# GpSimd writes a weight panel's high part with a copy in place of a product with ones, its loops written out

## What is computed

```python
def reference(x, ...):
    x = first_block(x, ...)    # stick-breaking attention, SwiGLU, gated side input
    x = second_block(x, ...)   # convolution of 31 taps and retention, in parallel
    return third_block(x, ...) # S5 and SSD state-space branches, gated side input

def swiglu(x, w_in, w_out):
    a, b = jnp.split(x @ w_in, 2, axis=-1)
    return (jax.nn.silu(a) * b) @ w_out
```

## Time and profile before

| | us |
|---|---|
| median of 3 runs (4802.05 to 4804.78) | 4803.22 |
| profiled execution, its own time | 4795.22 |
| its span, from the first to the last instruction | 4793.4 |
| TensorE busy (matmuls) | 4037.3 (84%) |
| VectorE busy | 2435.2 (51%) |
| GpSimd busy | 1553.4 (32%) |
| ScalarE busy | 881.2 (18%) |

### The profile page before, as it was taken

The page is one execution under the profiler, slowest core; times in us unless marked ns, Lnnn a source line. Parts: engine busy times, 40 slices in busy tenths (PEclk is TensorE's granted clock), DMA queues, the critical chain, the costliest instruction groups (busy, mean ns, idle before and its releaser), DMA issues.

```text
span 4793.4 us, 49704 instructions
## 1 busy us (share of the span) xinstructions
PE 4037.3 (84%) x19722; PEld 3259.1 (68%) x19722; DVE 2435.2 (51%) x2518; ACT 881.2 (18%) x1502; POOL 1553.4 (32%) x581
## 2 busy tenths in 40 slices
PE   7899998999999997777888895899896875559898
PEld 6677766877877875666665574678785764447677
DVE  3555556333333549877343324545249955543555
ACT  2433434100000221110001101112110111212021
POOL 1222222655556325555422130232223420004332
PEclk9999999999999988888999996988998976669899
DMA  1000000211111101111211111111831241112111
GB/s 68 27 27 23 23 27 31 66 58 65 53 60 63 36 27 52 58 61 57 70 44 49 48 44 44 48 53 62 143 78 55 90 135 27 26 26 83 66 40 57
DMA packets 139172, 260.00 MB, mean 54 GB/s; under 512 B 45584, under 2 KB 87568, under 8 KB 135952
## 3 DMA queue, kind: packets, MB, share of 16 engines
q1 hardware_dynamic: 47376, 143.67, 10.3%
q10 hardware_dynamic: 91648, 114.21, 7.3%
HBM read 209.35 MB, written 46.14 MB: 53 GB/s over the span
## 4 chain that ended last, share of the span: by engine, by line
PE 58%; DVE 16%; issue 15%; POOL 6%; ACT 3%; DMA 2%; ACTq 0%; SPq 0%; DVEq 0%; POOLq 0%
PE bank L514 15%; PE bank L515 14%; PE bank L516 14%; POOL wh L471 4%; PE bank L622 4%; POOL wl L473 2%; PE bank L751 1%; PE bank L714 1%; DVE xl L1610 1%; DVE spill L2098 1%; DVE hn L1599 1%; DVE fb L1737 1%; PE bank L984 1%; PE bank L734 1%; DVE gl L1774 1%
## 5 line engine op out<-in xcount | busy, mean ns | idle before, releaser
L471 POOL TENSOR_TENSOR wh<-raw,mats 128x1024 fp32r<-128x1024 f32 x264 | 739.5, 2801 | 3136.3 <-PE bank L516 3085.8
L514 PE MATMUL bank<-xh,wh 128*128 128x512 f32 x3008 | 1212.0, 403 | 279.6 <-DVE apad L1847 65.1
L515 PE MATMUL bank<-xl,wh 128*128 128x512 f32 x3008 | 1192.8, 397 | 0.0
L516 PE MATMUL bank<-xh,wl 128*128 128x512 f32 x3008 | 1190.6, 396 | 0.0
L514 PEld LDWEIGHTS bank<-xh,wh 128*128 128x128 f32 x3008 | 579.0, 192 | 445.3 <-issue 175.1
L473 POOL TENSOR_TENSOR wl<-raw,wh 128x1024 fp32r<-128x1024 f32 x264 | 697.4, 2642 | 20.7
L516 PEld LDWEIGHTS bank<-xh,wl 128*128 128x128 f32 x3008 | 577.8, 192 | 124.3
L515 PEld LDWEIGHTS bank<-xl,wh 128*128 128x128 f32 x3008 | 579.2, 193 | 115.6
L1867 DVE SCALAR_TENSOR_TENSOR cacc<-apad,cols,cacc 128x1024 f32<-128x1024 f32 x232 | 346.4, 1570 | 0.0
L1737 DVE TENSOR_TENSOR_SCAN fb<-fb 128x256 f32<-128x256 f32 (+7 forms) x128 | 209.5, 1677 | 102.8 <-ACT ab L1136 102.8
L1646 DVE TENSOR_TENSOR h<-bank,h 128x512 f32<-128x512 f32 x240 | 164.8, 691 | 188.9 <-PE bank L516 188.9
(11 more groups left out here) (324 smaller groups left out, 5691.1 us busy)
## 6 DMA issues: line engine op xcount, KB each, us to landing
raw<-in_wstream SPq DMA_DIRECT2D x264, 512.0 KB, 3.5
spills<-spill ACTq DMA_DIRECT2D x40, 512.0 KB, 2.7
rawm<-in_mod_w ACTq DMA_DIRECT2D x12, 1024.0 KB, 4.8
gate_spill<-gates ACTq DMA_DIRECT2D x16, 512.0 KB, 2.6
tabs<-in_rope ACTq DMA_DIRECT2D x4, 2048.0 KB, 7.6
f<-spills ACTq DMA_DIRECT2D x8, 1024.0 KB, 8.3
h<-in_x ACTq DMA_DIRECT2D x4, 1024.0 KB, 11.1
conv_spill<-cout ACTq DMA_DIRECT2D x8, 512.0 KB, 2.7
```

What stands on the lines that cost most here:

```text
L471: nc.gpsimd.tensor_tensor(wh[:, slot], raw[:, slot], ones, ALU.mult).then_inc(S("panel_high"), 1)
L514: nc.tensor.matmul(o, lh, rh, start=start, stop=False)
L515: nc.tensor.matmul(o, lh, rl, start=False, stop=False)
L516: return nc.tensor.matmul(o, ll, rh, start=False, stop=stop)
```

## The change

The high part of a panel, and of a modulation batch, is written by a copy from float32 to F32R; the constant ones and the wait for them at GpSimd's start go. GpSimd's hardware loop over the turns of a phase becomes a Python loop, so that all its splits stand in the program as plain instructions with constant waits. What waits for what is unchanged.

```diff
             nc.gpsimd.memset(eps[:, :], EPS).then_inc(S("eps"), 1)
-            ones = M["ones"].unsqueeze(1).broadcast_to([P, KT, P])
-            pool.wait_ge(S("setup"), 32)
...
-                nc.gpsimd.tensor_tensor(wh[:, slot], raw[:, slot], ones, ALU.mult).then_inc(S("panel_high"), 1)
+                nc.gpsimd.tensor_copy(wh[:, slot], raw[:, slot]).then_inc(S("panel_high"), 1)
                 pool.wait_ge(S("panel_high"), panel.value(1))
...
-                nc.gpsimd.tensor_tensor(w_high, w_raw, ones, ALU.mult).then_inc(S("mod_high"), 1)
+                nc.gpsimd.tensor_copy(w_high, w_raw).then_inc(S("mod_high"), 1)
...
                 if n > 1:
-                    with pool.Fori(1, n) as i:
+                    for i in range(1, n):
                         turn(name, i, [units(name, i) + (PANEL_UNITS[name][dp - 2 + m] - UNITS[name])
                                        for m in range(2)])
```

## The result

| | before | after |
|---|---|---|
| median, us | 4802.64 (4 runs) | 4661.2 (4 runs, 4653.9 to 4664.8) |
| profiled execution, its span | 4795.2, 4793.4 | 4664.7, 4662.9 |
| TensorE busy | 4037.3 | 4009.0 |
| VectorE busy | 2435.2 | 2234.3 |
| GpSimd busy | 1553.4 | 1156.7 |

The ratio is 0.9703, 95% interval [0.9686, 0.972]: 141 us faster. The likeliest case happened as described, but it brought nearly twice its price.

The account below looks back on a forecast made before the run. TensorE's waits for GpSimd's splits and for VectorE work slowed beside them were taken to bound the kernel. 61 copy savings of 1.17 us (71) plus 2 for loops took 4795.2 to 4722; 8.0 for the median gave 4730, range 4690 to 4820.

Parts of the forecast that it names:

- case A: Whole kernel: copy takes 1.2 us, short runs of convolution taps still shut GpSimd out; 4730 us, chance 0.60.
- the halving: GpSimd copy: if time goes with operands read, the product's (2.34 - 0.10) us halves, plus 0.10 start: 1.22 us.
- d: Every GpSimd split: what one copy saves against the product, taken as 1.17 us, with ends 0 and 1.31.
- 61 d: All stages: 24 + 4 certain savings of one copy plus 33 discounted ones, 61 x 1.17 = 71 us.
- The discount: Attention and other direct waits, feed-forward, state-space, output products: 7 + 10 + 19 + 8 = 44 savings, three quarters taken, 33.
- the ledger: Copy savings counted: convolution 24, retention 4, other direct waits 7, feed-forward 10, state-space 19, output products 8.
- The loops: GpSimd's written-out loops: half of 0.08 us saved as register work, some 50 splits on the path, 2 us.
- Each GpSimd operation is paid in full: State-space part, VectorE nearly always busy and bounding: 7 splits in 70 us and 12 in 180 us, 19 d.
- Case B: Convolution: copy gets between two taps, TensorE no longer waits for the panel; some 75 us more, 4655 us, chance 0.07.
- the request is of the same sort: Convolution, argument against the shut-out vanishing: all four short runs shut GpSimd out, one across some twenty taps.
- Case C: Convolution: short copy barely covers the run's first instruction, so subtraction waits for all taps; 4846 or 4817 us, chance 0.17.
- Cases D and E: GpSimd copy: D, runs at the product's pace, about 4800 us, chance 0.12; E, slower at 3 us, 4839, chance 0.04.

Follow-up runs that it names:

- the filled waits: Kernel before, with eight useless 128x512 matmuls ahead of TensorE's wait in the feed-forward output products: 4810.61 us, ratio 1.0025.
- the doubled copy: Changed kernel with each panel's copy made twice, one behind the other (not the modulation weights): 4709.53 us, ratio 0.9806.
- the halved product: Kernel before with GpSimd's loops written out and the product with ones made as two products of 128x512: 4763.83 us, ratio 0.9918.
- the gap at k=12: Changed kernel, but convolution tap k=12 on VectorE waits for the tap just before it, not the last but one: 4611.31 us, ratio 0.9608.
- The clean start: Changed kernel, but VectorE starts each run of taps only once the split under way is done: 4731.38 us, ratio 0.9841.
- the halved subtraction: Changed kernel with a dependent wait at tap k=12 and the subtraction made in two halves of 128x512: 4593.93 us, ratio 0.9578.

## Why the prediction was right and wrong, step by step

The mechanism was case A's, in all its signs. What failed is the sum that prices it: 73 us forecast, 141 measured. The largest single term is one that the sum put at nothing, the clock behind a wait (28.5 us measured).

**Which case.** Case A:

| sign | forecast | measured |
|---|---|---|
| copy, undisturbed | 1.1 to 1.3 us | 1.03 to 1.04 |
| long run, short run | 47.1, 34.8 us | 46.39, 34.76 |
| shut-out copy | near 24 us | 23.7 to 25.2 |
| wait for `apad` | 10.4 us, four times | 9.6, four times |
| wait for the split, convolution | 17.1 us | 50.9 in three, 17.0 |
| period | 119 us | 119.1 |
| wait in the retention | 4.1 us | 14.8 in four, 3.7 |
| idle in the S5 stretch | near 37 us | 60 - 22.90 = 37.1 |

The last three from TensorE's waits after, 1750 to 2224 and 2222 to 2880 us, and from the stretch that answers to the second of the earlier trace rows:

```profile
PE bank L512 <- POOL wl L471: 50.9, 3, 17.8
...
PE bank L512 <- POOL wl L471: 14.8, 4, 3.7
```

```profile
3570.00:3630.00 60.00, 22.90 (x95) 18.52 (x94) 58.15 (x55) 5.47 (x7) 8.78 (x4) 0.69 0.10 35
```

**The sum.** It gave 4722 for a profiled execution, and 4664.7 was measured, 57 us less. (The medians lie 69 us apart: the one execution was 8 us under its median before and 3.5 over it after, which I could not know.) Four terms make the 57:

1. The price of a copy. I took 1.2 us, the nearest value to ScalarE's 1.06 and the halving's 1.22; the copy takes 1.04, so that d is 2.37 - 1.04 = 1.33, not 1.17. On the 61 d that is 10 us. The saving is even a little beyond the end of 1.31 that I gave from ScalarE's row. From the Trainium skill (GPSIMD Engine Reference, section 3.1) I had worked out an estimate of 1.05 us, and the trace agrees: 1.04.
2. The discount. I cut 44 d to 33 "where a second wait may end a little later than the first". No wait took their place: TensorE's idle time fell by 101.9 us, and the undiscounted 72 d are 96. That is 11 d, 15 us, and 6 us beyond it, which no term explains. Stage by stage the ledger holds roughly: feed-forward 10 d = 13 for 16.5 us, convolution 24 d = 32 for 30.6, retention 4 d = 5 for 6.0, S5 19 d = 25 for 27.1. No row had spoken for the cut.
3. The clock. The sum has no such term: it took a shorter wait to be worth itself. The table shows 28.5 us of matmul time on top, 21.6 of it in attention and feed-forward, and for the feed-forward part the filled waits show that this comes from the idle time. The rows were there: the earlier trace rows have the clock at 0.63 in the stretch with the long wait, and matmuls of 0.79 us behind one of 18.29; I used the slow start only for cases B and C.
4. The loops: 2 us forecast, nothing that shows measured.

10 + 21 + 28 - 2 = 57. It closes by construction, since the second term takes what is left of the idle time.

**"Each GpSimd operation is paid in full"** was right for S5 as a sum, but I had taken what VectorE loses and what a split takes to be one quantity d. The doubled copy and the halved product show two. Where TensorE waits for the split (most of attention, retention, the shut-out's end), its whole length counts. Where VectorE meets GpSimd (feed-forward most clearly), the length of the one operation counts. The copy shortens both by the same 1.3 us, so that the sum didn't suffer, which is luck; for the doubled copy and the halved product it would have been wrong.

**Case B, the shut-out vanishes,** did not happen, and its argument against (the request is of the same sort) was right. Its price came out near: with the gap the convolution gains 81 us more against the changed kernel, where I had 75. But it had VectorE "still ready first", and it isn't: with the gap TensorE waits for `apad` in seven groups, 33.6 us. It also left out the next wait: 27 us go back in the retention.

**Case C, the shut-out spreads,** was given 0.17 and is wrong in its condition. It said that GpSimd gets in where its operation held up the run's first instruction. After the change L1861 takes an undisturbed 0.81 us. L1863, from 1885.13, is held up not by the copy, which ended at 1884.57, but by the subtraction behind it, which asked at 1884.64 during L1861; and the run is open. The kernel with the gap at k=12 has the reverse: L1861 held up for 2.27 us, and the run closed. The clean start shows one condition under which C happens: GpSimd's whole split over before the run begins. Then it happens, in all eight groups, and costs 70 us against the changed kernel. So C's mechanism exists; the change came nowhere near its point, since copy and subtraction together last 3.5 us and the run starts 0.87 us after the copy's start.

**Cases D and E** fell with the 1.04 us.

**The length of the shut-out.** The Trainium skill (SBUF - State Buffer, Who interferes with whom) has the second to issue blocked until the first instruction ends. In open runs the traces agree: the copy asked for at 1942.03 lasts 1.14 us where the next tap starts 0.16 us after the request. In closed runs they don't: 23.73 us behind some twenty taps, 29.98 behind 24. I gave B little because the product's 25.49 us spoke against the rule, and B did not happen.

## What to carry to other kernels

Before costing a shorter operation, write down who meets it: whoever waits for its result gains its whole time, whoever is held up beside it gains by the length of the single instruction, and splitting it in two gives part of the second gain (the halved product brought 38 us, the copy 141) at the cost of a longer whole. Where a TensorE wait becomes short, add the half-clock matmuls behind it, read from the duration of the matmuls that follow the wait in the timeline; where it stays long, add nothing. Discount a sum of waits only where a row shows what comes next. A long back-to-back series on VectorE can starve GpSimd for its whole length; one dependent wait, placed where GpSimd asks, opens it, but look first at what stands behind the stage, as a third to a half of such a gain went back there here.

## What the runs showed of the hardware that I had not expected

- A series of back-to-back VectorE taps has two behaviours, with the same instructions. Once GpSimd has come in, each of its operations comes in at the next end of a tap, and takes 1.1 to 3.5 us. If the series starts alone, GpSimd waits for its end, 23.7 to 30.0 us. A gap of 0.14 us between two taps lets a waiting operation in and leaves the series open. GpSimd at work at the start opens it in some cases only: not where the first instruction alone was held up (three series with the gap at k=12), and in the kernel with the halved subtraction not in two of four series in which the second instruction was (1.76 to 1.78 us in place of 0.75). What decides is not shown: each tap starts 73 to 81 ns before the last one's recorded end in the open runs of the kernels before, after and with the clean start, 75 to 91 in the closed ones, so that the spacing of a single tap doesn't tell them apart.
- GpSimd's copy from float32 to F32R takes 1.04 us for 128x1024, the product with ones 2.34 to 2.42, the subtraction the same. Two products of 128x512 beside a busy VectorE took 3.00 us together, one undisturbed 1.27.
- Nine waits of nearly the same length (2.25 to 2.32 us) in the same place of a loop were followed by half clock four times only. What decides it stays open.
